# State-space scan: the decay matrices of both directions added on GpSimd before one multiplication

## What is computed

```
    seg = jnp.exp(jnp.where(tril, acum[:, :, :, None] - acum[:, :, None], -jnp.inf))
    cb = jnp.einsum('bcign,bcjgn->bcijg', cm, bm)
    y_intra = jnp.einsum('bcijgr,bcjgrp->bcigrp', seg * cb[..., None], v)
...
    o_f, s_f = scan_fn(*args_f, init_f, with_out)
    o_b, s_b = scan_fn(*[flip(a) for a in args_b], init_b, with_out)
    o = o_f + flip(o_b) if with_out else None
...
    y = (y_ssd + ssd_d.astype(F32)[:, None] * xs).reshape(bsz, t, SSD_INNER) * jax.nn.silu(z.astype(F32))
```

## Time and profile before

| | us |
|---|---|
| median of 3 runs (2188.45 to 2189.74) | 2189.33 |
| span of the profiled execution, first to last instruction | 2185.7 |
| PE busy in the span | 1882.4 |
| the scan, first spread to first mean | 442.6 to 539.0 |
| PE, DVE, ACT, POOL busy in the scan | 89.5, 52.0, 40.0, 21.8 |

### The profile page before, as it was taken

One profiled execution on the slowest core, in us unless ns is written; L12 is line 12 of the kernel. 1 busy time (PEld: TensorE's weight loads), 2 busy tenths in 40 slices (PEclk: granted clock), 3 DMA queues, 4 the chain that ended last, 5 costly groups with the idle time before them and its releaser, 6 DMA issues.

```text
span 2185.7 us, 32921 instructions
## 1 busy us (share of the span) xinstructions
PE 1882.4 (86%) x14024; PEld 1132.1 (52%) x14024; DVE 804.4 (37%) x1427; ACT 507.6 (23%) x1119; POOL 335.2 (15%) x323
## 2 busy tenths in 40 slices
PE   6999889999999998888889999989999975666565
PEld 3874668745875433333236556677787731212112
DVE  3331757555633010000026877566774300000001
ACT  2452321343012100001023323444442100000001
POOL 1431054322320000000013000054540000000000
PEclk9999999999999999999999999999999998878888
DMA  9321031240239999999993433200004699999997
GB/s 385 142 86 73 5 118 78 119 190 1 89 150 384 428 430 426 429 431 431 428 407 147 169 154 140 103 2 2 2 2 174 233 428 429 430 427 432 430 430 298
DMA packets 46689, 528.07 MB, mean 242 GB/s; under 512 B 3408, under 2 KB 7760, under 8 KB 23120
## 3 DMA queue, kind: packets, MB, share of 16 engines
q1 hardware_dynamic: 44784, 522.56, 57.3%
q10 hardware_dynamic: 1760, 3.42, 0.4%
HBM read 524.91 MB, written 1.05 MB: 241 GB/s over the span
## 4 chain that ended last, share of the span: by engine, by line
PE 53%; DMA 28%; DVE 12%; issue 2%; ACT 2%; DVEq 1%; PEld 1%; PEldq 0%; POOLq 0%; POOL 0%; ACTq 0%; SPq 0%
DMA ring<-in_moe_w 27%; PE bank L1435 12%; PE bank L709 8%; PE bank L820 7%; PE bank L1317 4%; PE bank L1250 3%; PE bank L788 3%; DVE ring L2421 2%; DVE x L2280 2%; PE bank L1036 2%; PE bank L1013 2%; DVE x L2859 1%; PE bank L961 1%; DMA ring<-in_mod_w 1%; PE bank L627 1%
## 5 line engine op out<-in xcount | busy, mean ns | idle before, releaser
L1435 PE MATMUL bank<-ring,xgs 128*32 128x512 f32 x2984 | 374.0, 655 | 129.4 <-DMA ring<-in_moe_w 128.0
L1435 PEld LDWEIGHTS bank<-ring,xgs 128*32 128x32 f32 x2984 | 106.3, 119 | 370.6 <-issue 284.9
L1435 PE MATMUL bank<-ring,hT 128*32 128x512 f32 x1488 | 190.1, 663 | 75.3 <-DMA ring<-in_moe_w 75.1
L820 PE MATMUL bank<-hT,ring 128*128 128x256 f32 (+1 forms) x784 | 232.7, 454 | 2.0 <-ACT hT L1607 1.4
L2700 DVE SCALAR_TENSOR_TENSOR x<-bank,modT,x 128x256 f32<-128x256 f32 x96 | 42.4, 480 | 457.1 <-PE bank L1461 456.9
L820 PEld LDWEIGHTS bank<-hT,ring 128*128 128x128 f32 x784 | 146.6, 190 | 82.3 <-issue 66.8
L1435 PEld LDWEIGHTS bank<-ring,hT 128*32 128x32 f32 x1488 | 52.3, 120 | 199.3 <-issue 152.6
L2280 DVE SCALAR_TENSOR_TENSOR x<-gluR,cols,x 128x256 f32<-128x256 f32 x240 | 116.2, 484 | 16.6 <-issue 0.9
L709 PE MATMUL bank<-hT,ring 128*128 128x256 f32 x432 | 99.9, 381 | 3.7 <-ACT ssd_g L1658 2.2
L709 PEld LDWEIGHTS bank<-hT,ring 128*128 128x128 f32 x432 | 81.1, 190 | 17.9 <-issue 6.2
L3091 POOL MEMSET gluR<- 128x3008 f32 x1 | 2.6, 2610 | 498.9 <-DVEq L2710 498.9
(11 more groups left out here) (573 smaller groups left out, 3026.0 us busy)
## 6 DMA issues: line engine op xcount, KB each, us to landing
ring<-in_moe_w SPq DMA_DIRECT2D x56, 4096.0 KB, 22.8
ring<-in_moe_w SPq DMA_DIRECT2D x28, 2048.0 KB, 21.1
ring<-in_moe_w SPq DMA_DIRECT2D x55, 1024.0 KB, 14.4
ring<-in_mod_w SPq DMA_DIRECT2D x12, 4096.0 KB, 13.4
ring<-in_moe_w SPq DMA_DIRECT2D x12, 3072.0 KB, 22.0
ring<-in_cd_w SPq DMA_DIRECT2D x6, 4096.0 KB, 14.1
ring<-in_ab_w SPq DMA_DIRECT2D x5, 4096.0 KB, 15.3
ring<-in_ab_wo SPq DMA_DIRECT2D x2, 4096.0 KB, 14.9
```

The source lines that it names most:

```text
L820: last = mm(ps[p["no"] % 4][:, p["c0"]:T], w[:, k, :], hT[:, k, p["c0"]:T], start=(k == 0), stop=(k == KD - 1))
L1435: last = mm(ps[banks + s][32 * j:32 * j + 32, :], lhs[s][:, 4 * kh + k, 32 * j:32 * j + 32], piece(g, k, j), start=(kh == 0 and k == 0), s ...
```

## The change

For each head GpSimd adds the two directions' matrices in place (`both_ways`), DVE multiplies the sum by C.B once, and PE has one product for both directions beside that for the skip. Per pair `outputs` issues 16 matmuls where it issued 24, tile by tile, one tile a step, one step later than before. On PE it now stands ahead of `item_add`. Both weight sums of `mix_out` move from behind the scan into POOL's steps 9 and 12. Three entries each of `SSD_ACC` and `SSD_EVAC` move by one step. Two waits of PE, for `gla_zeroed` and `routed`, go away. The cut diff:

```diff
-        SSD_ACC = {z: v for v, z in enumerate([-2, 0, 2, 4, 6, 8, 16, 17, 19, 21, 23, 25])}
+        SSD_ACC = {z: v for v, z in enumerate([-2, 0, 2, 4, 6, 8, 17, 18, 19, 21, 23, 25])}
...
                 def outputs(k, q):
-                    for n in range(3 * q, 3 * q + 3):
-                        kind, t = n // 4, n % 4
-                        if kind and t == 0:
-                            pe.wait_ge(sg("ssd_mat"), 4 * k + 2 + kind)
-                        for hp in range(2):
...
+                    if q == 0:
+                        pe.wait_ge(sg("ssd_skip"), 1 + k // 4)
+                        pe.wait_ge(sg("ssd_mat"), 2 * k + 2)
+                    for hp in range(2):
+                        mm(ps[k % 4][half, tiles[q]], xs_t[:, k, q, half], dskI[:, 2 * k + hp, :],
...
+                    for hp in range(2):
+                        last = mm(ps[k % 4][half, tiles[q]], xs_t[:, k, q, half], mats[(4 * k + 2 * hp) % 8][:, tiles[q]],
...
-                    for d in range(2):
-                        u = 4 * k + 2 * hp + d
-                        dve.wait_ge(sg("ssd_decay"), u + 1)
-                        V.tensor_tensor(mats[u % 8], mats[u % 8], cbs[k // 4], ALU.mult).then_inc(sg("ssd_mat"), 1)
+                    m = mats[(4 * k + 2 * hp) % 8]
+                    dve.wait_ge(sg("ssd_both"), 2 * k + hp + 1)
+                    V.tensor_tensor(m, m, cbs[k // 4], ALU.mult).then_inc(sg("ssd_mat"), 1)
...
+                def both_ways(k, hp):
+                    u = 4 * k + 2 * hp
+                    pool.wait_ge(sg("ssd_decay"), u + 2)
+                    G.tensor_tensor(mats[u % 8], mats[u % 8], mats[u % 8 + 1], ALU.add).then_inc(sg("ssd_both"), 1)
+                for z in range(-6, 32):
+                    k, q = z // 4, z % 4
+                    if z + 2 in SSD_KV:
+                        item_values(SSD_KV[z + 2])
+                    if z in (-6, 9):
+                        skip_blocks(int(z == 9))
+                    if z >= -4 and q in (1, 2):
+                        both_ways(k + 1, q - 1)
+                    if z in (9, 12):
+                        mix_out(OUT_MIX[z == 12:][:1])
...
-            mix_out()
+            mix_out(OUT_MIX[2:])
```

More of the change, by code:

```diff
@@ L946, in outputs @@
                 def outputs(k, q):
-                    if k < 0:
+                    if not 0 <= k < 8:
                         return
-                    if k == 0 and q == 0:
-                        pe.wait_ge(sg("ssd_skip"), 1)
-                    if k == 4 and q == 0:
-                        pe.wait_ge(sg("ssd_skip"), 2)
-                    for n in range(3 * q, 3 * q + 3):
-                        kind, t = n // 4, n % 4
-                        if kind and t == 0:
-                            pe.wait_ge(sg("ssd_mat"), 4 * k + 2 + kind)
-                        for hp in range(2):
-                            half = slice(64 * hp, 64 * hp + 64)
-                            right = mats[(4 * k + 2 * hp + kind - 1) % 8][:, tiles[t]] if kind else dskI[:, 2 * k + hp, :]
-                            last = mm(ps[k % 4][half, tiles[t]], xs_t[:, k, t, half], right, start=False, stop=True,
-                                      skip_group_check=True, tile_position=(0, 64 * hp))
+                    if q == 0:
+                        pe.wait_ge(sg("ssd_skip"), 1 + k // 4)
+                        pe.wait_ge(sg("ssd_mat"), 2 * k + 2)
+                    for hp in range(2):
+                        half = slice(64 * hp, 64 * hp + 64)
+                        mm(ps[k % 4][half, tiles[q]], xs_t[:, k, q, half], dskI[:, 2 * k + hp, :],
+                           start=False, stop=True, skip_group_check=True, tile_position=(0, 64 * hp))
+                    for hp in range(2):
+                        half = slice(64 * hp, 64 * hp + 64)
+                        last = mm(ps[k % 4][half, tiles[q]], xs_t[:, k, q, half], mats[(4 * k + 2 * hp) % 8][:, tiles[q]],
+                                  start=False, stop=True, skip_group_check=True, tile_position=(0, 64 * hp))
                     if q == 3:
@@ L970, in ssd @@
                 pe.wait_ge(sg("ssd_cbm"), 2)
-                for z in range(-4, 32):
+                for z in range(-4, 33):
                     k, q = z // 4, z % 4
@@ L1452, in scatter @@
                     done = Q * layer + q
-                    if q == 0 and steps[0] == 0:
-                        pe.wait_ge(sg("routed"), layer + 1)
                     for dt in steps:
@@ L1545, in _ @@
             project_gla()
-            pe.wait_ge(sg("gla_zeroed"), 1)
             pe.wait_ge(sg("proj_evacuated"), copied(GLA_PAIRS, 0))
@@ L2181, in gla_begin @@
                 V.memset(attm[:, :, :, :], 0.0)
-                dve.drain().then_inc(sg("gla_zeroed"), 1)
+                dve.drain()
                 dve.wait_ge(sg("gla_gz"), 2 * GH)
@@ L2824, in scale @@
                     dve.drain().then_inc(sg("head_mixed"), 1)
-                for z in range(-4, 33):
+                for z in range(-4, 34):
                     k, q = z // 4, z % 4
@@ L2980, in mix_h, with mix_out @@
                     pool.drain().then_inc(sg("weights_mixed"), 1)
-            def mix_out():
-                for v, n in OUT_MIX:
+            def mix_out(steps):
+                for v, n in steps:
                     wa, wb = out_weights(2 * v), out_weights(2 * v + 1)
```

17 lines of the change are left out of this document (8 added, 9 removed).

## The result

| | before | after |
|---|---|---|
| median us (range) | 2189.4 (2186.19 to 2193.04) | 2194.86 (2191.82 to 2198.48) |
| ratio, 95% interval | | 1.0025 (1.0013 to 1.0036) |
| span of the profiled execution | 2185.7 | 2193.5 |
| the scan, POOL's first values to first mean | 96.41 | 103.17 |

The changed kernel is 0.25% slower. That is 5.5 us by the medians, where I had forecast 2.8; the time lies inside the range of 2187.0 to 2196.0. By my bound of 0.2% this is slower and not the same, though the interval holds the bound. So the outcome to which I had given 0.26 came about, and not the one with 0.60, which ended at 2193.7. The two profiled executions are 7.8 us apart.

The account below looks back on a forecast made before the run. PE, busy for 89.5 of the scan's 96.4 us, was taken to bound it. +2.5 at kv(7), -1.6 from there to the first mean and +1.9 for the clock gave +2.8 on 2189.33: 2192.1 us, range 2187.0 to 2196.0.

Parts of the forecast that it names:

- the outcome to which I had given 0.26: Whole kernel: slower beyond the 0.2% bound, through slow additions on POOL, 2196.1 us; chance 0.26.
- the one with 0.60: Whole kernel: no measurable change, POOL's queue paying out at kv(7) what PE saved, 2188.8 to 2193.7 us; chance 0.60.
- The total passes on the scan: Behind the scan: whatever the scan gains or loses, seen at the first mean's start, goes into the total one for one.
- Durations on POOL: POOL in the scan: addition 1.22 us, weight sum 2.31 back to back, a multiplication slipping in costs 0.44.
- the additions are slow: Rival, POOL's additions in the scan: 1.73 instead of 1.22 us each, +4.0 on the forecast, 2196.1 us; chance 0.26.
- The new wait at kv(7): PE at kv(7): POOL's full queue delays DVE's scaling, kv(7) +2.5 us later, PE standing some 6 us.
- PE's work: PE's outputs in the scan: 128 records fewer save 7.0 us, five more groups cost 0.75, net 6.2 us off.
- From kv(7) to the first mean: Later part of the scan, without the clock: -2.7 for fewer records, +0.4 and +0.6, sum -1.6 us.
- The +0.6 at the end: End of the scan: last outputs follow the fourth sum of squares, and the last gate follows them before the mean: +0.6 us.
- the +0.4 at kv(9): PE at kv(9): it now waits for two additions on POOL as well, +0.4 us.
- The clock: PE behind kv(7): a wait of 6 us brings a stretch at 1.2 GHz costing 1.3 to 2.6, taken as +1.9 us.
- The rival that POOL keeps up: POOL ahead of kv(7): pair 4's second addition done in time, PE's saving comes through, 2182.4 to 2183.7 us; chance 0.14.

Follow-up runs that it names:

- e3: The changed kernel without the 16 additions on GpSimd, so part of the output is missing; weight sums stay in the scan: 2186.42 us, ratio 0.9986.
- e5: The changed kernel with both weight sums behind the scan, started only after VectorE's last multiplication of decay matrices: 2190.54 us, ratio 1.0008.
- e2: The changed kernel with ten unread 128x128 identity multiplications put on PE ahead of kv(7) to keep it busy: 2192.76 us, ratio 1.0019.
- e8: e5 with the outputs of a step moved ahead of its spreads and kv: 2186.77 us, ratio 0.9989.
- e12: The changed kernel with one edit alone, the outputs of a step ahead of its spreads and kv: 2187.19 us, ratio 0.9989.
- e7: e3 with the outputs at the step and place of the kernel before, one step earlier and behind the item additions: 2183.33 us, ratio 0.9975.
- e4: The kernel before with only the two weight sums moved to where the changed kernel has them: 2191.30 us, ratio 1.0013.
- e1: The changed kernel with the two weight sums taken out of GpSimd's queue in the scan and put back behind it: 2192.31 us, ratio 1.0018.
- e13: e5 with the outputs at the step and place of the kernel before and the additions on VectorE: 2187.47 us, ratio 0.9989.

## Why the prediction was right, and where it was wrong

**The total passes on the scan.** Right: from the first mean to the end 1645.8 us, 1646.7 before, and in all the kernels between 1643.4 and 1648.4. To within some 2.5 us, then, which is as much as several of the differences between versions.

**Durations on POOL.** Right. The additions took 1.26 to 1.34 alone, the weight sum 2.35, and an addition into which a multiplication slipped 1.73, 0.47 more than alone where I had charged 0.44. So the rival *the additions are slow* did not come about, though its 2196.1 us lies close to the result: time alone would have spoken for it.

**The new wait at kv(7).** Right in mechanism and place: +3.0 us against +2.5. POOL's queue ran without a pause and was as long as forecast (12.45 us from 484.49 to the end of pair 4's additions, against 12.4); it began 0.8 later than I had put it. kv(1) came 0.8 later, where I had 0.9. Wrong was the wait of PE, 3.42 and not some 6 us, and for a reason that leads to the next point: PE came to kv(7) 51.7 us after the scan's start, not 48.4. The spread for pair 4 had taken 2.4 us instead of 1.06, and 3.41 us at the low clock cost some more.

**PE's work.** Here a step failed. "Net 6.2 us off PE" holds for the outputs (18.04 in e3, 24.28 before), but the same reordering put 4.1 us onto their neighbours. I had seen that "ACT now awaits" the outputs one step later and charged it at pair 3 alone, as 0.59 us; I counted the change of shape for the outputs' own groups and not for the kv, far halves and additions beside them.

**From kv(7) to the first mean.** The same error: forecast -1.6 without the clock. At the full clock it was 0.0 to -0.1 (e3, e5, and e2 after taking off half of 3.2). The +0.6 at the end came (kv(11) to the last gate 17.8, 17.2 before), the +0.4 at kv(9) did not (a wait of 0.94 before and after). With the outputs ahead of the spreads it is -2.6 (e8, e12), and with the old order and no additions -3.0 (e7). So the -2.7 for the records was there to be had, and the place of the outputs took it.

**The clock.** The place was right and the size was off. I took 1.9 us; in the profiled execution 8.65 us at half speed stood behind kv(7), 4.3 us, and e2, where that shrank, confirms that it is paid. That the length of the wait brings it, as I had argued, the runs do not bear out (e4, and the last section). My source for the size, the low stretches behind two other waits, were 2.7 to 5.2 us; this one was longer, behind a shorter wait.

**The sum.** +3.0 at kv(7), -0.1 to -0.5 behind it and +4.3 for the clock make the 6.8 to 7.2 of the scan; the medians, over several executions, say 5.5. I had +2.5, -1.6 and +1.9. All three were off in one direction, by 0.5, some 1.3 and 2.4, and the range held since it had been drawn to a slow rival that did not happen. That is luck in part.

**The rival that POOL keeps up.** I made both weight sums its condition. e5 took both out, and the last addition of pair 4 ended 1.9 us earlier, not 4 to 5, and kv(7) came 1.9 earlier, and the total went to 2190.5, not 2183. Behind POOL's queue stood ACT's exponentials and DVE's order, which I had not followed for that case.

## What to carry to other kernels

When an edit takes work from the engine that sets the pace and moves the rest of it in the order, price the neighbours too: who waits for the moved work (here ACT, through a buffer of two pairs), and which instructions now stand beside a matmul of another shape. An edit that seems to fail may be right and only in the wrong place: here one line, the outputs ahead of the spreads, was worth 7.7 us, more than the whole change had lost, though about half of that came through the clock. And a sum of two tensors that VectorE can add in 0.69 us right ahead of its next step need not gain by GpSimd, whose 1.26 us come with a handover and hold VectorE up: on VectorE it was faster in the old order, and not told apart with the outputs first.

## What the runs showed of the hardware that I had not expected

- In the scan the clock fell in every profiled execution with additions and in none without (before, e3, e4, e7 at 1.00), but not by the length of a wait alone. e4's wait of 2.85 us left it at 1.00, and e12's of 2.89 was followed by 0.54 for 7.36 us. In after it fell at 491.27, where PE's rows of the 15 us ahead show no idle time over 0.3 us; PE stood in that spread, though, for 1.4 us in all, which its modelled ends partly hide. e1 and e5 show the same fall at the same place, e2, alike up to there, does not. What decides it stays open.
- The same wait of PE of 4.78 us ahead of the scan was followed by 6.83 us at 1.2 GHz in the execution of before and by 10.24 in that of after, and by 6.8 again in e12 and e13, whose code up to there is that of after. From the end of that wait to POOL's first values it is 151.6 us in the six executions with 6.83 (before, e2, e4, e8, e12, e13) and 153.5 or 153.6 in the four with 10.24 (after, e1, e5, e7). So this, and not the dropped wait, is 1.9 of the 2.0 us by which the scan of after begins later. In all the kernels the start lay between 442.3 and 445.0, and a comparison of two spans can be off by that much. The two stretches, before and after:

```profile
289.31:296.14 6.83, 4.54 (x21) 4.17 (x21) 5.72 (x10) 0.00 (x0) 1.45 (x2) 0.50 1.02 413
...
289.88:300.12 10.24, 8.39 (x29) 7.31 (x30) 5.38 (x11) 0.02 (x1) 1.03 (x3) 0.50 0.84 339
```

- VectorE and GpSimd shut each other out for the whole of an instruction: a multiplication of 0.69 us that began 0.09 us behind a weight sum took 2.82 (e1), and one that began 0.08 behind it 2.82 (after). By the Trainium skill (SBUF — State Buffer, SBUF: two separate sides) a DVE instruction with two inputs in SBUF and a GpSimd instruction that reads SBUF exclude each other for the whole instruction; these rows agree. A GpSimd addition into which a multiplication slipped took 1.73 instead of 1.27 (after).
- Work of another tile shape took longer on both sides of a group of outputs: the additions of an item 1.05 us elsewhere and 1.16 behind outputs, as the timelines of e8 and e3 show, and the far half of a spread, from its start to the next work, 0.44 elsewhere and 0.54 ahead of outputs, in before as in after. That the shape is the reason, and not something else about the outputs, no run separates.

```profile
463.04 1.05 PE L942 MATMUL bank<-ident,hT 128*128 128x128 f32 x8
```

```profile
462.05 1.16 PE L942 MATMUL bank<-ident,hT 128*128 128x128 f32 x8
```
